# FFN output products: one more seven-product group in each second pass, T2's weight sum moved to an adding DMA, T4's kept on VectorE, products reordered

## The chip, the core and the metric

One core of a Trainium2 chip runs the whole program. The metric is the device time of one execution in microseconds; the median of three runs of the kernel before is 1753.33 us. TensorE is the matrix engine, VectorE and ScalarE work elementwise, GpSimd issues some DMAs, and SyncE (SP in the profile) issues most loads.

## What is computed

A decoder layer on 256 tokens of width 2048 in float32: a SwiGLU FFN, a token mixer, a second SwiGLU FFN. Only the output products of the two FFNs change (`D_FF` = 5504 = 43 k-tiles of 128):

```python
def swiglu_ffn(x, w_in, w_out):
    gate, up = jnp.split(x @ w_in, 2, axis=-1)
    return (jax.nn.silu(gate) * up) @ w_out

x = x + 0.5 * swiglu_ffn(rmsnorm(x, ffn1_norm[l]), ffn1_w_in[l], ffn1_w_out[l])
...
x = x + 0.5 * swiglu_ffn(rmsnorm(x, ffn2_norm[l]), ffn2_w_in[l], ffn2_w_out[l])
```

## The kernel before

**Split numbers.** A float32 product is made of three matmuls of rounded parts: high x high, high x low, low x high. ScalarE copies a weight tile into the ring `whi` (high part), VectorE subtracts it from the original into `wlo` (low part), then TensorE takes both. The same is done with the activations `act` (`act_hi`/`act_lo` into `aw_hi`/`aw_lo`, one k-tile of 128x256; `group_act_hi`/`group_act_lo` for a group's two pairs of tiles). The ring has `SLOTS` = 4 slots (L40) in this stage, so ScalarE's copy for product h waits until TensorE has used product h - 4 (`weights_used`).

**Output stage** (`ffn_out`, once per FFN u = 0, 1). It has two passes c = 0, 1, each over 1024 of the 2048 output columns and all 43 k-tiles. A "plain" item is one k-tile: 2 token blocks x 2 column blocks x 3 = 12 matmuls of 512 columns. Four k-tiles can form a group instead: the 2x2 by 2x2 block product is done with seven products instead of eight (a scheme of Winograd's kind). Each of the seven ("T1", "B11", "T3", "T2", "B21", "B22", "T4") is 2 k-tiles x 3 = 6 matmuls, so a group takes 42 matmuls, four plain tiles 48. The T products need sums of weight blocks (`out_sum`, four 128x1024 operations of VectorE per group), and T1, T2, T3 and B22 need sums of activation blocks (`group_form_sums`, four 128x256 operations, then one copy and one low part of 128x1024, `group_form_hi` and `group_form_lo`). The sums of activations are made in the first pass only and kept in `sfo` for the second one.

**Order.** `out_items` (L65) lists the items of a pass; all three engines walk this list. Both passes have four groups. With P for a plain tile a first pass runs

```text
P P P P P P | T1 B11 P T3 T2 P B21 B22 P T4 P P | T1 B11 ... T4 P P | ... T4 P P P
```

and a second pass has five leading and four trailing P. Work of VectorE between the items is placed by position: `group_form_sums` six items ahead of T1, `group_form_lo` three ahead, `out_sum` T1 two ahead. After the last T4 of a pass, six `join` steps add the separate accumulators onto x (`copy_p1` on ScalarE ahead of them). TensorE starts the second pass after join step 2. In the second FFN the last three plain tiles are done bank by bank, and ahead of them TensorE waits for `aw_ready` of the very last tile (L844).

**Loads.** `out_loads` (L84) orders the loads of weight pieces (1 MB each: two k-tiles of 1024 columns). Plain pieces use three slots, group pieces (two per group, n0 with B11 and B12, n1 with B21 and B22) three others. SyncE's queue is in order; `free` names what must be done before a slot is filled again: for n0 the sum for T4, for n1 the low part of B22. GpSimd's queue carries, in this stage, the reload of x, and at the end of the first FFN the small loads of the mixer. In the FFN input stage GpSimd already issues adding DMAs (`add_piece`, L599).

## Time and profile before

| | |
|---|---|
| median of 3 runs | 1753.33 us (1752.81 to 1753.72) |
| profiled execution | 1753.02 us, span of the profile 1751.2 us |
| TensorE busy | 1742.3 us (99%) |
| VectorE busy | 1473.4 us (84%) |
| ScalarE busy | 1106.5 us (63%) |
| granted TensorE clock | 1.000 of full speed |
| DMA | 405.03 MB, mean 231 GB/s |

The output stages run from 456.4 to 681 us (first FFN) and from 1524 to 1748 us (second FFN). The timeline has a row for an instruction: start, duration, engine, source line, operation, tiles, and in brackets how long the engine was idle before it and what released it. Durations overlap in a pipeline: what an instruction costs its engine is the distance from its start to the next one's.

### The profile page before, as it was taken

To read this page: it belongs to the slowest core of one execution; us is meant where nothing else is said; L and a number is where in the kernel's file an instruction comes from. 1 tells how busy PE (TensorE), PEld (TensorE's weight loads), DVE (VectorE), ACT (ScalarE), POOL (GpSimd) and SP (SyncE) were. 2 spreads that over 40 slices of the span, in tenths; PEclk is the share of its full clock that TensorE was granted. 3 is DMA by queue.
4 is the path that set the end of the run, shared out by engine and by line. 5 is a ranking of instruction groups with operands and counts; after the bars stand their busy time and mean duration, and the time that the engine had idled before them with its cause. 6 is when DMAs were issued, how large, how long until landed. Compare 5 with 4: busy or idle time off the path is not lost.

```text
span 1751.2 us, 21435 instructions
## 1 busy us (share of the span) xinstructions
PE 1742.3 (99%) x7976; PEld 1451.8 (83%) x7976; DVE 1473.4 (84%) x1778; ACT 1106.5 (63%) x1461; POOL 94.9 (5%) x111
## 2 busy tenths in 40 slices
PE   9999999999999999999999999999999999999999
PEld 7888888888888888888888888888888888988887
DVE  7999889998999998575655655898999898899998
ACT  7676666766666666454545554667676676666665
POOL 0000100000000001100000000010000000000000
PEclk9999999999999999999999999999999999999999
DMA  9899899997555556555454558689999898764762
GB/s 378 255 294 275 260 264 265 265 277 236 210 212 201 197 215 210 186 186 178 160 185 161 176 175 298 207 264 263 267 277 278 272 282 239 251 210 159 257 218 90
DMA packets 168327, 405.03 MB, mean 231 GB/s; under 512 B 9016, under 2 KB 18000, under 8 KB 162848
## 3 DMA queue, kind: packets, MB, share of 16 engines
q1 hardware_dynamic: 154208, 342.03, 54.3%
q0 software_dynamic: 12896, 59.67, 17.2%
q10 hardware_dynamic: 1120, 1.97, 0.3%
q8 instruction: 64, 1.05, 0.2%
q14 instruction: 39, 0.32, 0.0%
HBM read 351.57 MB, written 5.79 MB: 204 GB/s over the span
## 4 chain that ended last, share of the span: by engine, by line
PE 95%; DVE 3%; DMA 1%; ACT 0%; issue 0%; SPq 0%; POOL 0%; DVEq 0%; ACTq 0%
PE bank L699 8%; PE bank L700 8%; PE bank L701 8%; PE bank L726 8%; PE bank L728 7%; PE bank L727 7%; PE bank L660 7%; PE bank L662 7%; PE bank L661 7%; PE bank L806 5%; PE bank L808 5%; PE bank L807 5%; PE bank L833 3%; PE bank L834 3%; PE bank L832 3%; DVE wlo L1363 1%
## 5 line engine op out<-in xcount | busy, mean ns | idle before, releaser
L1363 DVE TENSOR_TENSOR wlo<-raw,whi 128x1024 fp32r<-128x1024 f32 (+1 forms) x466 | 559.8, 1208 | 179.4 <-ACT whi L1002 173.6
L1002 ACT ACTIVATE whi<-raw 128x1024 fp32r<-128x1024 f32 (+1 forms) x466 | 486.3, 1047 | 304.1 <-PE bank L662 189.2
L726 PE MATMUL bank<-whi,xs 128*128 128x512 f32 (+1 forms) x528 | 205.6, 389 | 3.0 <-DVE wlo L1363 2.3
L728 PE MATMUL bank<-whi,xs 128*128 128x512 f32 (+1 forms) x528 | 203.1, 385 | 0.0
L727 PE MATMUL bank<-wlo,xs 128*128 128x512 f32 (+1 forms) x528 | 202.9, 384 | 0.0
L806 PE MATMUL bank<-whi,aw_hi 128*128 128x512 f32 x420 | 164.0, 390 | 0.0
L808 PE MATMUL bank<-whi,aw_lo 128*128 128x512 f32 x420 | 163.5, 389 | 0.0
L807 PE MATMUL bank<-wlo,aw_hi 128*128 128x512 f32 x420 | 163.4, 389 | 0.0
L660 PE MATMUL bank<-whi,xs 128*128 128x512 f32 x384 | 155.1, 404 | 0.4 <-DVE wlo L1363 0.4
L662 PE MATMUL bank<-whi,xs 128*128 128x512 f32 x384 | 150.0, 391 | 0.0
L661 PE MATMUL bank<-wlo,xs 128*128 128x512 f32 x384 | 149.5, 389 | 0.0
L1002 ACT ACTIVATE whi<-tsum 128x1024 fp32r<-128x1024 f32 (+1 forms) x96 | 96.9, 1032 | 43.2 <-DMA tmini<-minis 14.8
L1227 ACT ACTIVATE whi<-raw 128x1024 fp32r<-128x1024 f32 x80 | 84.7, 1059 | 61.1 <-PE bank L808 37.0
L726 PEld LDWEIGHTS bank<-whi,xs 128*128 128x128 f32 x528 | 99.2, 188 | 24.6 <-ACT p1s L1170 2.1
L701 PE MATMUL bank<-whi,xs 128*128 128x512 f32 (+1 forms) x312 | 119.3, 382 | 0.0
L699 PE MATMUL bank<-whi,xs 128*128 128x512 f32 (+1 forms) x312 | 119.3, 382 | 0.0
L700 PE MATMUL bank<-wlo,xs 128*128 128x512 f32 (+1 forms) x312 | 119.3, 382 | 0.0
L728 PEld LDWEIGHTS bank<-whi,xs 128*128 128x128 f32 x528 | 99.1, 188 | 19.1
L1363 DVE TENSOR_TENSOR wlo<-tsum,whi 128x1024 fp32r<-128x1024 f32 (+1 forms) x96 | 111.2, 1187 | 3.8 <-ACT whi L1002 3.8
L727 PEld LDWEIGHTS bank<-wlo,xs 128*128 128x128 f32 x528 | 99.4, 188 | 18.0
L699 PE MATMUL bank<-whi,sf 128*128 128x512 f32 (+1 forms) x260 | 99.6, 383 | 0.0
L701 PE MATMUL bank<-whi,sf 128*128 128x512 f32 (+1 forms) x260 | 99.4, 382 | 0.0
(257 smaller groups left out, 3541.6 us busy)
## 6 DMA issues: line engine op xcount, KB each, us to landing
raw<-ffn_w_in SPq DMA_DIRECT2D x86, 1024.0 KB, 6.8
raw<-ffn_w_out SPq DMA_DIRECT2D x84, 1024.0 KB, 6.4
raw<-w_in SPq DMA_DIRECT2D x48, 1024.0 KB, 5.0
raw<-ffn_w_in SPq DMA_DIRECT2D x75, 512.0 KB, 7.4
tsum<-raw POOLq DMA_DIRECT2D x35, 1024.0 KB, 7.9
minis<-ffn_w_in SPq DMA_DIRECT2D x72, 256.0 KB, 7.5
last_plain<-ffn_w_in SPq DMA_DIRECT2D x36, 512.0 KB, 9.3
raw<-w_out SPq DMA_DIRECT2D x16, 1024.0 KB, 5.0
```

Source lines behind the costliest of these rows:

```text
L660: mm(banks[b][:, 0:w], stationary[:, k, 0, tok], hi, start=k == 0, stop=False, skip_group_check=True)
L661: mm(banks[b][:, 0:w], stationary[:, k, 0, tok], lo, start=False, stop=False, skip_group_check=True)
L662: last = mm(banks[b][:, 0:w], stationary[:, k, 1, tok], hi, start=False, stop=k == k_total - 1, skip_group_check=True)
L699: mm(bank_out[:, 0:w], st_hi, hi, start=start, stop=False, skip_group_check=True)
L700: mm(bank_out[:, 0:w], st_hi, lo, start=False, stop=False, skip_group_check=True)
L701: return mm(bank_out[:, 0:w], st_lo, hi, start=False, stop=stop, skip_group_check=True)
L726: mm(banks[b][:, 0:w], xs[:, k + i, 0, tok], hi, start=starts[b] and k + i == 0, stop=False, skip_group_check=True)
L727: mm(banks[b][:, 0:w], xs[:, k + i, 0, tok], lo, start=False, stop=False, skip_group_check=True)
L728: last = mm(banks[b][:, 0:w], xs[:, k + i, 1, tok], hi, start=False, stop=k + i == last_k, skip_group_check=True)
L806: mm(bank_out[:], st_hi, hi, start=i == 0, stop=False, skip_group_check=True)
L1002: A(hi_of(h)[:, 0:n_el], src, ACT.Copy).then_inc(weights_hi, 1)
L1363: V.tensor_tensor(lo_of(h)[:, 0:n_el], src, hi_of(h)[:, 0:n_el].bitcast(f32), ALU.subtract).then_inc(weights_lo, 1)
```

## The change

The second pass of each FFN gets a fifth group (k-tiles 16 to 19, which stay plain tiles in the first pass). Its sums of activations are made in the second pass and take the place of group 0's in `sfo`. The sum for T2 is made by an adding DMA that GpSimd issues, in the buffer that holds the sum for T1 (there are two such buffers, by turns); the sum for T4 is added by VectorE in the same buffer. All weight sums become additions, and the signs move to the sums of activations and to the last join steps. T2 and B22 change places, and T4 of a group is done behind T1 and B11 of the next group. The second pass has no plain tiles between its groups:

```text
first pass, new:   P P P P P P | T1 B11 P T3 B22 P T2 B21 P P P | T1 B11 T4' P T3 B22 P T2 B21 P P P | ... B21 P | T4 P P P
second pass, new:  P P P P P | T1 B11 P T3 B22 P T2 B21 P | T1 B11 T4' P T3 B22 P T2 B21 P | ... five groups ... B21 P | T4 P P P
```

(T4' is the T4 of the group before.) The activations of B11 are split for one token block only, those of B21 and T4 at B22. Slot n0 is free after the low part of T3, n1 after that of T4. The join steps are packed closer together.

```diff
-OUT_GROUPS = (4, 4)
+GROUP_IDS = ((0, 1, 2, 3), (0, 1, 2, 3, 4))
+OUT_GROUPS = tuple(len(ids) for ids in GROUP_IDS)
-LEADS = ((6, 2, 2, 2), (5, 2, 2, 2))
+LEADS, BETWEEN = (6, 5), (2, 0)
+KEPT = 4
+SUMS_AT = [(0, g) for g in range(OUT_GROUPS[0])] + [(1, KEPT)]
...
+        items += [("form", g, "T1"), ("form", g, "B11")] + ([("form", g - 1, "T4")] if g else [])
+        for forms in (("T3", "B22"), ("T2", "B21"), ()):
+            items += [("plain", next(plain))] + [("form", g, f) for f in forms]
+        items += [("plain", next(plain)) for _ in range(BETWEEN[c] if g + 1 < OUT_GROUPS[c] else 0)]
+    return items + [("form", OUT_GROUPS[c] - 1, "T4")] + [("plain", k) for k in plain]
...
+JOIN_FROM = [OUT_ITEMS[c].index(("form", OUT_GROUPS[c] - 1, "T2")) + 4 for c in range(PASSES)]
+JOIN_STEPS = [{JOIN_FROM[0]: (0,), JOIN_FROM[0] + 1: (1, 2)},
+              {JOIN_FROM[1]: (0,), JOIN_FROM[1] + 1: (1, 2), JOIN_FROM[1] + 2: (3,)}]
...
-            at.setdefault(-(-done // 2) + 1 if g else 1, []).append(g)
+            at.setdefault(done // 2 + 2 if g else 1, []).append(g)
...
-                        if q < 2 * OUT_GROUPS[c] and q % 2 == 0:
-                            return out_sums, 4 * group(u, c, q // 2) + 4
-                        item = ("form", q // 2, "B22") if q < 2 * OUT_GROUPS[c] else ("plain", min(2 * q + 1, FT - 1))
+                        item = ("form", q // 2, ("T3", "T4")[q % 2]) if q < 2 * OUT_GROUPS[c] else ("plain", min(2 * q + 1, FT - 1))
...
+            def out_adds(u):
+                for c in range(PASSES):
+                    for g in range(OUT_GROUPS[c]):
+                        G, n1 = group(u, c, g), out_piece(u, c, 2 * g + 1)
+                        pool.wait_ge(weights_lo, out_half(u, c, ("form", g, "T1")) + 1)
+                        pool.wait_ge(raw_full[raw_slot(n1)], RAW_FULL[n1])
+                        pool.dma_start(out_half_sum(G), quarter(n1, 1), accum_op=ALU.add).then_inc(out_t2, 16)
...
             x_again(0)
+            out_adds(0)
...
+                            if f == "T2":
+                                act_e.wait_ge(out_t2, 16 * (G + 1))
+                            if f == "T4":
+                                act_e.wait_ge(out_t4, G + 1)
...
-                            if f in ("T1", "B11"):
-                                group_act_hi(u, c, g, (0,) if f == "T1" else (1,))
+                            if f in ("T1", "B22"):
+                                group_act_hi(u, c, g, 0 if f == "T1" else 1)
...
-                if f == "T2":
-                    dve.wait_ge(out_sums, 4 * G + 2)
-                    dve.wait_ge(weights_lo, out_half(u, c, ("form", g, "B11")) + 1)
-                    V.tensor_tensor(B11, B12, B11, ALU.add).then_inc(out_sums, 1)
                 if f == "T4":
-                    dve.wait_ge(out_sums, 4 * G + 3)
-                    V.tensor_tensor(pair(tsum[:, 2 * W:4 * W]), B21, B11, ALU.subtract).then_inc(out_sums, 1)
+                    dve.wait_ge(weights_lo, out_half(u, c, ("form", g, "T2")) + 1)
+                    V.tensor_tensor(out_half_sum(G), quarter(n1, 0), out_half_sum(G), ALU.add).then_inc(out_t4, 1)
...
-                                if d == (5 if g1 else 3) and c1 == 0:
-                                    group_form_sums(u, 0, g1)
-                                if d == 2 and c1 == 0:
-                                    group_form_lo(u, 0, g1)
+                                if d == (5 if g1 else 3) and (c1, g1) in SUMS_AT:
+                                    group_form_sums(u, c1, g1)
+                                if d == 2 and (c1, g1) in SUMS_AT:
+                                    group_form_lo(u, c1, g1)
```

## Rows read from the trace of the kernel before

**Rows 1.** The page, chain of work that ended last, by engine.
```profile
PE 95%; DVE 3%; DMA 1%; ACT 0%; issue 0%; SPq 0%; POOL 0%; DVEq 0%; ACTq 0%
```

**Rows 2.** Timeline of TensorE, 1714 to 1719 us: start, duration, instruction.
```profile
1715.78 0.39 PE L806 MATMUL bank<-whi,aw_hi 128*128 128x512 f32 x1
...
1718.50 0.39 PE L806 MATMUL bank<-whi,aw_hi 128*128 128x512 f32 x1
```

**Rows 3.** Windows (first and second pass): us, then PE, PEld, DVE, ACT, POOL busy.
```profile
500.00:530.00 30.00, 30.00 (x134) 24.86 (x133) 29.97 (x37) 20.81 (x27) 0.00 (x0) 1.00 0.52 191
600.00:640.00 40.00, 40.00 (x178) 33.12 (x177) 37.71 (x41) 25.84 (x33) 0.00 (x0) 1.00 0.57 210
```

**Rows 4.** Timeline of VectorE and TensorE, first pass, 529 to 546 us.
```profile
529.11 0.42 DVE L1457 TENSOR_TENSOR gset<-act 128x256 f32<-128x256 f32 x1
...
530.58 1.22 DVE L1679 TENSOR_TENSOR wlo<-raw,whi 128x1024 fp32r<-128x1024 f32 x1
...
540.67 0.68 DVE L1445 TENSOR_TENSOR aw_lo<-act,aw_hi 128x512 fp32r<-128x512 f32 x1
541.27 1.22 DVE L1477 TENSOR_TENSOR raw<-raw 128x1024 f32<-128x1024 f32 x1
542.40 1.22 DVE L1679 TENSOR_TENSOR wlo<-raw,whi 128x1024 fp32r<-128x1024 f32 x1
...
544.14 0.42 DVE L1440 TENSOR_TENSOR aw_lo<-act,aw_hi 128x256 fp32r<-128x256 f32 x1
544.48 1.22 DVE L1363 TENSOR_TENSOR wlo<-raw,whi 128x1024 fp32r<-128x1024 f32 x1
...
545.84 0.47 PE L806 MATMUL bank<-whi,aw_hi 128*128 128x512 f32 x1
```

**Rows 5.** Timeline of ScalarE and TensorE: pitch of copies, and a copy behind TensorE.
```profile
547.83 0.40 ACT L1066 ACTIVATE aw_hi<-act 128x256 fp32r<-128x256 f32 x1
548.14 1.05 ACT L1002 ACTIVATE whi<-raw 128x1024 fp32r<-128x1024 f32 x1
...
1718.95 0.39 PE L808 MATMUL bank<-whi,aw_lo 128*128 128x512 f32 x1
...
1719.43 1.06 ACT L1227 ACTIVATE whi<-raw 128x1024 fp32r<-128x1024 f32 x1 [1.66 <-PE bank L808]
```

**Rows 6.** Timeline of all engines at the end of the last pass, 1728 to 1740.
```profile
1728.56 0.58 ACT L1086 ACTIVATE p1s<-bank 128x512 f32<-128x512 f32 x1
...
1730.32 1.06 ACT L1227 ACTIVATE whi<-tsum 128x1024 fp32r<-128x1024 f32 x1 [1.18 <-PE bank L808]
...
1731.41 1.23 DVE L1679 TENSOR_TENSOR wlo<-tsum,whi 128x1024 fp32r<-128x1024 f32 x1 [1.44 <-ACT whi L1227]
...
1738.16 1.28 DVE L1495 SCALAR_TENSOR_TENSOR x<-bank,x 128x512 f32<-128x512 f32 x2
...
1739.35 0.39 PE L808 MATMUL bank<-whi,aw_lo 128*128 128x512 f32 x1
1739.36 0.41 DVE L1440 TENSOR_TENSOR aw_lo<-act,aw_hi 128x256 fp32r<-128x256 f32 x1
...
1739.83 0.50 PE L861 MATMUL bank<-whi,aw_hi 128*128 128x512 f32 x1
```

**Rows 7.** Adding DMAs of GpSimd in the input stages: issues, and landing of L603.
```profile
L603 POOL DMA_DIRECT2D tsum<-raw x37: 847/856/940, 71.5 to 1489.5; - x37
...
DMA to landing us min/median/max: 5.6/7.9/9.7
...
tsum<-raw POOLq DMA_DIRECT2D x35, 1024.0 KB, 7.9
...
tmini<-minis POOLq DMA_DIRECT2D x35, 256.0 KB, 9.4
...
1284.73 0.86 POOL L603 DMA_DIRECT2D tsum<-raw  x1 [22.46 <-DVE wlo L1369]
1285.27 1.20 POOL L604 DMA_DIRECT2D tmini<-minis  x1
```

**Rows 8.** Weight loads issued between 562 and 570 us, time to landing.
```profile
DMA to landing us min/median/max: 7.7/9.1/10.5
```

**Rows 9.** Timeline of VectorE behind the first FFN's output stage.
```profile
679.87 1.66 DVE L1379 SCALAR_TENSOR_TENSOR xs<-bank,gains,xs 128x256 fp32r<-128x256 f32 x4 [3.71 <-ACT xs L1022]
```

More of the change, by code:

```diff
@@ L53 @@
 FIRST_OUT_SLOT = 2
-OUT_GROUPS = (4, 4)
+GROUP_IDS = ((0, 1, 2, 3), (0, 1, 2, 3, 4))
+OUT_GROUPS = tuple(len(ids) for ids in GROUP_IDS)
 OUT_PLAIN = [4 * g for g in OUT_GROUPS]
-FORMS = ("T1", "B11", "T3", "T2", "B21", "B22", "T4")
-LEADS = ((6, 2, 2, 2), (5, 2, 2, 2))
+LEADS, BETWEEN = (6, 5), (2, 0)
+KEPT = 4
+SUMS_AT = [(0, g) for g in range(OUT_GROUPS[0])] + [(1, KEPT)]
 def out_items(c):
-    items, plain = [], iter(range(OUT_PLAIN[c], FT))
+    plain = iter(range(OUT_PLAIN[c], FT))
+    items = [("plain", next(plain)) for _ in range(LEADS[c])]
     for g in range(OUT_GROUPS[c]):
-        items += [("plain", next(plain)) for _ in range(LEADS[c][g])]
-        for forms in (("T1", "B11"), ("T3", "T2"), ("B21", "B22"), ("T4",)):
-            items += [("form", g, f) for f in forms]
-            if forms != ("T4",):
-                items.append(("plain", next(plain)))
-    return items + [("plain", k) for k in plain]
+        items += [("form", g, "T1"), ("form", g, "B11")] + ([("form", g - 1, "T4")] if g else [])
[3 more added lines that the diff above has]
+    return items + [("form", OUT_GROUPS[c] - 1, "T4")] + [("plain", k) for k in plain]
 OUT_ITEMS = [out_items(c) for c in range(PASSES)]
@@ L78 @@
 OUT_AT = [0, OUT_LEN[0]]
-T4_ENDS = [OUT_ITEMS[c].index(("form", OUT_GROUPS[c] - 1, "T4")) for c in range(PASSES)]
+JOIN_FROM = [OUT_ITEMS[c].index(("form", OUT_GROUPS[c] - 1, "T2")) + 4 for c in range(PASSES)]
+JOIN_STEPS = [{JOIN_FROM[0]: (0,), JOIN_FROM[0] + 1: (1, 2)},
+              {JOIN_FROM[1]: (0,), JOIN_FROM[1] + 1: (1, 2), JOIN_FROM[1] + 2: (3,)}]
 ACT_PLAIN = [ACT_PAIRS - 2 * g for g in OUT_GROUPS]
@@ L169, in raw_slot @@
     if n >= IN_P[1]:
-        return (0, 2, 1, 3, 4, 5, 0, 1)[n - IN_P[1]]
+        oldest = (FIRST_OUT_SLOT - sum(ACT_PLAIN) - (IN_P[1] - QKV_P)) % QKV_RAW_SLOTS
+        return (*((oldest - i) % QKV_RAW_SLOTS for i in range(3)), 3, 4, 5, 0, 1)[n - IN_P[1]]
     return (FIRST_OUT_SLOT - sum(ACT_PLAIN) - (n - QKV_P)) % QKV_RAW_SLOTS if n >= QKV_P else n % RAW_SLOTS
@@ L376, in split_sums, with out_half_sum, kept @@
         def split_sums(g):
-            return sfo[:, 4 * g:4 * g + 4]
-        def kept(u, g):
-            return OUT_GROUPS[1] * u + g + 1
+            return sfo[:, 4 * (g % KEPT):4 * (g % KEPT) + 4]
+        def out_half_sum(G):
+            return pair(tsum[:, 2 * W * (G % 2):2 * W * (G % 2 + 1)])
+        def kept(u, c, g):
+            last = max(i for i, (c1, g1) in enumerate(SUMS_AT) if (c1, g1) <= (c, g) and g1 % KEPT == g % KEPT)
+            return len(SUMS_AT) * u + last + 1
         p_banks = [bank[0:4], bank[4:8]]
@@ L1070, in group_act_hi @@
                     c0, g0 = (c, g - 1) if g else (c - 1, OUT_GROUPS[0] - 1)
[L1071 removed]
+                    act_e.wait_ge(weights_used, out_half(u, c0, ("form", g0, ("B11", "T4")[part])) + 1)
                 else:
                     act_e.wait_ge(weights_used, unit_half(u, UNITS - 1) + B22 + 2)
[L1074 to L1076 removed]
+                t, cols = 4 * GROUP_IDS[c][g] + 2 * part, (P, SEQ)[part]
+                act_e.wait_ge(act_copied, ACT_PAIRS * u + t // 2 + 1)
+                A(aw_hi[:, 2 + part, :, 0:cols], act[:, t:t + 2, 0:cols], ACT.Copy).then_inc(ga_hi, 1)
             def group_form_hi(u, c, g):
[L1079 to L1080 removed]
+                act_e.wait_ge(weights_used, out_half(u, c, ("form", g - KEPT, "T2")) + 1 if g >= KEPT else OUT[u])
+                act_e.wait_ge(gs_summed, 4 * kept(u, c, g))
                 A(split_sums(g)[:, :, :, 0, :], gs[c], ACT.Copy).then_inc(gs_hi, 1)
@@ L1209, in ffn_out @@
                         if len(ahead) > 3 and ahead[3][0] == "form" and ahead[3][2] == "T1":
-                            if c == 0 and i + 3 < OUT_LEN[0]:
-                                group_form_hi(u, 0, ahead[3][1])
+                            if (c, ahead[3][1]) in SUMS_AT and i + 3 < OUT_LEN[c]:
+                                group_form_hi(u, c, ahead[3][1])
                         if item[0] == "plain":
@@ L1675, in ffn_out @@
                             n0, n1 = out_piece(u, c, 2 * g), out_piece(u, c, 2 * g + 1)
-                            src = {"T1": pair(tsum[:, 0:2 * W]), "B11": quarter(n0, 0), "T3": quarter(n0, 1), "T2": quarter(n0, 0),
-                                   "B21": quarter(n1, 0), "B22": quarter(n1, 1), "T4": pair(tsum[:, 2 * W:4 * W])}[f]
+                            own = out_half_sum(group(u, c, g))
+                            src = {"T1": own, "B11": quarter(n0, 0), "T3": quarter(n0, 1), "T2": own,
+                                   "B21": quarter(n1, 0), "B22": quarter(n1, 1), "T4": own}[f]
                             dve.wait_ge(weights_hi, h + 1)
```

82 lines of the change are left out of this document (38 added, 44 removed).

## Prediction

> **What bounds the kernel now.** I read the chain of waits first: 95% of the time to the end is TensorE work [rows 1], so only fewer products, or a wait of TensorE, can move the time. The page's mean of one matmul (0.389 us) is no price: matmuls overlap. The timeline gives it: twelve matmuls of 512 columns start in 2.72 us (1715.78 to 1718.50), 0.2267 us each [rows 2]. A plain k-tile (12 matmuls) is 2.72 us of TensorE, a form product (6) 1.36 us.
>
> Then I asked who is nearly late. In the windows of the output stage TensorE is busy without a break, but VectorE nearly is too: 29.97 of 30 us in the first pass, 37.71 of 40 in the second [rows 3]. The timeline of VectorE gives the prices, by the distance from one start to the next [rows 4]: a 128x1024 operation (a low part, or a sum of weights) 1.13 us (541.27 to 542.40), the activations' low part of a plain tile 0.34 (544.14 to 544.48), that of 128x512 0.60 (540.67 to 541.27), the four sums of activations 1.47 (529.11 to 530.58). In a first-pass group of five plain tiles and seven forms VectorE has 12 low parts (13.6), 5 x 0.34, 2 x 0.60, 4 sums of weights (4.5), 1.47 and 1.13 for the sums of activations: 23.6 us, against 5 x 2.72 + 7 x 1.36 = 23.1 on TensorE. It loses half a microsecond per group, and in the fourth its lead is used up: the low part begun at 544.48 ends at 545.70, and the matmul that needs it starts at 545.84 and is the slow first one, 0.47 us [rows 4]. No time is lost there yet, but the stage has no slack that a denser order could use.
>
> How far may VectorE run ahead? ScalarE may copy into a ring slot when TensorE has used the product four before it. Such a copy starts 0.25 us after the next product began (last matmul of the product started at 1718.95, so the next product at 1719.18, and the copy at 1719.43) [rows 5]; the low part starts 1.09 us after the copy (1730.32, 1731.41) [rows 6] and takes 1.22. So a low part is ready 2.5 to 2.6 us after the product four before it, if VectorE is free.
>
> **The change part by part.**
> (a) The fifth group: four k-tiles (48 matmuls) become seven forms (42). Two second passes: 12 matmuls fewer, 12 x 0.2267 = **-2.72 us**.
> (b) T2's sum leaves VectorE: -1.13 us per group there, worth nothing by itself, since TensorE did not wait. First pass: 23.6 - 1.13 - 0.26 (the first group copy is half as wide) = 22.2 against 23.1: the tight place at 545.84 goes, and no time with it.
> (c) The second pass has no plain tiles between its groups any more. A group is 3 plain tiles and 7 forms: TensorE 8.16 + 9.52 = 17.7 us. VectorE: 10 low parts 11.3, 3 x 0.34, 0.34 + 0.60, 3 sums 3.4: 16.7. It fits, at 94%. But group 4 was not summed in the first pass. Its sums (1.47) and their low part (1.13) fall inside group 3: 19.3 against 17.7. I follow the one stretch in which VectorE has no gap. It starts behind the low part of B21 of group 2, which is ready 2.5 us after the product four before it (T3 of group 2) is used. From there VectorE does: sum T1, sum T4, low parts of plain, T1, B11, T4, plain, T3, sum T3 (9 x 1.13 = 10.2) and three small ones (1.0), 11.2 in all; then the sums of activations 1.47, low parts B22, plain, T2, the form sums, B21, sum T1, sum T4, plain (8 x 1.13 = 9.1), 0.60 and two of 0.34: 11.8. With 0.2 for the end of the last one and the hand-over: 2.5 + 11.2 + 11.8 + 0.2 = 25.7 us. TensorE meanwhile has B22, plain, T2, B21, plain, T1, B11, T4, plain, T3, B22, plain, T2, B21: 10 forms and 4 plain, 13.6 + 10.9 = 24.5, and wants the last plain tile of group 3. **It waits 1.3 us, in each of the two stages: +2.6.**
> (d) The end. Before its last section (three tiles, bank by bank) TensorE waits for the activations' low part of the very last tile. Before, TensorE had T4 and a plain tile to do in front of it, and still waited: last matmul at 1739.35, the next due at 1739.58, that low part begun at 1739.36, matmul at 1739.83, 0.25 us [rows 6]. Now T4 stands last and the plain tile in front of it is gone. After T2 of group 4 is used: 0.25, ScalarE's copy of P1 (0.5 of its 0.58 us [rows 6]), the tile's activations 0.31 (547.83 to 548.14 [rows 5]), the copy, 2.1 us to VectorE's low part; then 1.13, join 0.60, 0.34, 1.13, three joins 1.8 (two took 1.20 from 1738.16 to 1739.36 [rows 6]), 0.42: 7.6. TensorE has B21, plain, T4: 5.4. Wait 2.2, less the 0.25 of before: **+1.9**, once, in the second FFN. In the first, the next work needs no such wait, and VectorE, which stood idle for 3.71 us before 679.87 [rows 9], takes the same lateness out of that cover; without it, it would cost up to the same 1.9.
> (e) T2's sum as a DMA. GpSimd waits for T1's low part and the piece's landing; behind it on its queue stand only the next sums and, in the first FFN, the small loads of the mixer, not due for some 30 us. ScalarE's copy of T2 waits for the landing, and all later copies with it. No half-size adding DMA is in the trace. From above: 1 MB landed in 7.9 us (5.6 to 9.7), an issue 0.86 [rows 7]; from below, 256 KB more landed about 2 us later (issue 0.54 after, 9.4 to land), so 8 us per MB and perhaps 4 for half. I take 6. The window: T2's copy is due when the plain tile behind B11 is used; from T1's gate to that are 5 forms and 2 plain, 12.2 us, plus 0.25, less 2.6 for T1's own low part and about 0.8 of VectorE's queue: 9 us. Cost 0, as long as it lands within 9 us; the whole measured span but its end does.
> (f) Loads. The group's second piece is held until T4's low part, three products into the next group; its first one is freed at T3. SP's queue is in order, so the plain piece behind them waits too. The first piece is used 8 us after T3, the second 11 or more; loads landed in 7.7 to 10.5 us where several were queued [rows 8]. Three in a row are issued from 1.4 us before T3. I take 0 and keep +1 per stage.
>
> The profiled execution took 1753.02 us (span 1751.2 and 1.8 around it), 0.3 under the median: -2.72 + 2.6 + 1.9 = +1.8, so 1754.8 on it, and **1755.1** on the median of 1753.33.
>
> A page's rule against (e): the Trainium skill ("SBUF — State Buffer", who interferes with whom) says that a VectorE instruction with two SBUF inputs excludes a GpSimd instruction that reads SBUF. In the units GpSimd's issues beside a busy VectorE took 0.86 us each [rows 7]; no row shows one beside a VectorE at 100%. Another page ("DMA: Bandwidth & Descriptors", anatomy of one DMA) gives 2 us + bytes/436 GB/s, an estimate of 3.2 us for 512 KB; for the 1 MB of [rows 7] it would give 4.4, and the trace says 7.9. By either figure the sum stays.
>
> **The rivals.**
> *Only the products count*: VectorE makes up the 1.3 and the 1.9 somewhere, because a stretch that I took as gapless is shorter. For it: none of 16 groups of before lost time, and (b) gives VectorE 1.13 per group. Against it: both are sums of one queue's own durations. 1753.3 - 2.7 = 1750.6; with one of the two waits 1752 to 1753.
> *The adding DMA is late* (slower). It decides from a landing 9 to 10 us after T1's low part. Behind T2's gate VectorE has T2, B21, two sums and a plain tile, 6.0 us and 1.4 for the copy, TensorE 8.2: 0.8 us of slack in second-pass groups. At 11 us, 2 late, each of 10 groups loses 1.2: 12 us, 1767. At 10, some 2 us: 1757. For it: the 9.7 of [rows 7], loads beside it, and the rule on SBUF above. Against: half the bytes.
> *Loads late in the dense pass*: +1 to +1.5 per stage, 1757 to 1758. For it: the 10.5 of [rows 8].
> *More than the products is gained*: the 0.25 of the end and stalls that I can't see go: below 1749.8.
>
> **How the numbers follow.** A run of this kernel can tell 0.2% (3.5 us) from no change. Forecast 0.55 (own range 1753.8 to 1756.8); products only 0.16; DMA late 0.14; loads late 0.11; more gained 0.04. Faster than 1749.8: 0.04. Slower than 1756.8: most of the late DMA and of the late loads and the forecast's edge, 0.12 + 0.09 + 0.05 = 0.26. The rest, 0.70, is within. The range: 1750.3 (products only, less 0.3) to 1759.5 (loads late, or a DMA at 10.3 us), leaving out 0.05 below and 0.1 above.
>
> **What would show it.** (a) 12 matmuls fewer, starts still 0.2267 us apart. (c) in each second pass one gap on TensorE of about 1.3 us in front of the plain tile that follows B21 of group 3, released by VectorE's low part, VectorE without a gap for 23 us ahead of it. (d) a gap of 2.2 us in front of the last section, released by the activations' low part. (e) the adding DMA of 512 KB lands in 4 to 8 us and ScalarE never waits for it. (b) VectorE under 29 of 30 us in the first pass. I am wrong if gaps stand in front of T2 or in every group (then the DMA or the loads), or if those two gaps are missing.

## The result, and the profile after

The changed kernel takes 1761.05 us (median of 6 executions, 1758.86 to 1764.51), the kernel before 1753.53 beside it: 1.0046 times as long, 95% interval 1.0032 to 1.0059. The forecast was 1755.1 with a range to 1759.5. The profiled execution took 1759.58 us (span 1757.3, clock 1.000), so by its own sum the prediction (1754.8 on the profiled execution) is 4.8 us short, and the median lies another 1.5 above. The result is outside the range, on the slow side.

The page of the changed kernel, busy times (us, share of the span, count), then the chain that ended last by engine:

```profile
PE 1740.6 (99%) x7964; PEld 1449.5 (82%) x7964; DVE 1470.4 (84%) x1780; ACT 1111.4 (63%) x1465; POOL 116.5 (7%) x129
...
PE 88%; DVE 7%; DMA 3%; issue 1%; ACT 1%; SPq 0%; POOL 0%; DVEq 0%; ACTq 0%
```

TensorE has 12 matmuls fewer (7976 before) and is busy for less time than before (1742.3 us); the span is 6.1 us longer. The chain, 95% TensorE before [rows 1], is now 88% TensorE, 7% VectorE and 3% DMA (3% and 1% before). So TensorE waits. The page of waits says for what:

```profile
PE bank L825 <- DVE wlo L1386: 5.9, 4, 1.7
...
PE bank L880 <- DVE aw_lo L1463: 2.0, 1, 2.0
```

Four waits for a plain tile's low part, one for the activations' low part in front of the last section. The timeline of TensorE, each time the last matmul ahead of a gap and the one behind it (start, duration, instruction, idle and releaser); 0.2267 us is the step from start to start without a gap [rows 2]:

```profile
649.07 0.39 PE L853 MATMUL bank<-whi,aw_lo 128*128 128x512 f32 x1
650.74 0.47 PE L825 MATMUL bank<-whi,aw_hi 128*128 128x512 f32 x1 [1.28 <-DVE wlo L1386]
...
1663.31 0.39 PE L853 MATMUL bank<-whi,aw_lo 128*128 128x512 f32 x1
1665.31 0.47 PE L825 MATMUL bank<-whi,aw_hi 128*128 128x512 f32 x1 [1.61 <-DVE wlo L1386]
...
1700.57 0.39 PE L853 MATMUL bank<-whi,aw_lo 128*128 128x512 f32 x1
1702.64 0.47 PE L825 MATMUL bank<-whi,aw_hi 128*128 128x512 f32 x1 [1.68 <-DVE wlo L1386]
...
1720.20 0.39 PE L853 MATMUL bank<-whi,aw_lo 128*128 128x512 f32 x1
1721.94 0.47 PE L825 MATMUL bank<-whi,aw_hi 128*128 128x512 f32 x1 [1.35 <-DVE wlo L1386]
...
1743.60 0.39 PE L853 MATMUL bank<-whi,aw_lo 128*128 128x512 f32 x1
1745.94 0.50 PE L880 MATMUL bank<-whi,aw_hi 128*128 128x512 f32 x1 [1.96 <-DVE aw_lo L1463]
```

The time lost is the distance of the two starts less 0.2267. Three of the five were forecast, with their places: 650.74 (1.44 us) and 1721.94 (1.51) for the last plain tile of group 3, and 1745.94 (2.11) for the last section. Two were not: 1665.31 (1.77) and 1702.64 (1.84), both in the second FFN only. "DVE wlo" as releaser hides their cause; VectorE's own timeline has it:

```profile
1661.34 1.23 DVE L1496 TENSOR_TENSOR tsum<-raw 128x1024 f32<-128x1024 f32 x1 [2.07 <-DMA raw<-ffn_w_out]
1662.48 1.22 DVE L1503 TENSOR_TENSOR tsum<-raw,tsum 128x1024 f32<-128x1024 f32 x1
1663.61 0.42 DVE L1463 TENSOR_TENSOR aw_lo<-act,aw_hi 128x256 fp32r<-128x256 f32 x1
1663.95 1.22 DVE L1386 TENSOR_TENSOR wlo<-raw,whi 128x1024 fp32r<-128x1024 f32 x1
...
1698.66 1.23 DVE L1496 TENSOR_TENSOR tsum<-raw 128x1024 f32<-128x1024 f32 x1 [2.15 <-DMA raw<-ffn_w_out]
```

VectorE stands idle for 2.07 and 2.15 us in front of the sum for T1 of the next group, because the group's first piece has not landed. Behind that sum stand T4's sum and the low part of the plain tile, and TensorE wants that plain tile first. The loads are issued by SyncE three in a row; the view of line L491 for the stretches 1648 to 1656 and 1688 to 1696 us:

```profile
L491 SPq DMA_DIRECT2D raw<-ffn_w_out x3: 367/368/469, 1651.6 to 1652.7; - x3
...
DMA to landing us min/median/max: 7.0/9.3/11.1
...
L491 SPq DMA_DIRECT2D raw<-ffn_w_out x3: 368/368/403, 1689.0 to 1690.1; - x3
...
DMA to landing us min/median/max: 6.2/9.2/11.0
```

The order in the queue is a plain piece, the group's first piece, its second. The middle one, issued at 1651.97, lands 9.3 us later, at 1661.31: that is when the sum starts. VectorE was ready for it 7.3 us after the issue (7.0 us at the second place). Groups 1 and 3 have such a triple; for groups 2 and 4 the plain piece came earlier. The first FFN's second pass has the same two triples; there the middle load landed in 7.3 and 7.2 us, and VectorE did not wait.

### The profile page after: what moved, and what is told of

The parts are those of the page before. It is cut to its first block, busy times and chain, and to the rows that moved or that the text cites. A ratio compares the mean times of both kernels' runs of the same rounds, so it can differ in the third digit from the quotient of the medians.

```text
span 1757.3 us, 21439 instructions
## 1 busy us (share of the span) xinstructions
PE 1740.6 (99%) x7964; PEld 1449.5 (82%) x7964; DVE 1470.4 (84%) x1780; ACT 1111.4 (63%) x1465; POOL 116.5 (7%) x129
## 3 DMA queue, kind: packets, MB, share of 16 engines
q8 instruction: 64, 1.05, 0.2%
## 4 chain that ended last, share of the span: by engine, by line
PE 88%; DVE 7%; DMA 3%; issue 1%; ACT 1%; SPq 0%; POOL 0%; DVEq 0%; ACTq 0%
PE bank L718 8%; PE bank L720 8%; PE bank L719 8%; PE bank L745 8%; PE bank L747 7%; PE bank L746 7%; PE bank L679 7%; PE bank L681 7%; PE bank L680 7%; PE bank L825 4%; PE bank L827 4%; PE bank L826 4%; PE bank L853 2%; PE bank L852 2%; PE bank L851 2%; DMA raw<-ffn_w_out 2%
## 5 line engine op out<-in xcount | busy, mean ns | idle before, releaser
L1386 DVE TENSOR_TENSOR wlo<-raw,whi 128x1024 fp32r<-128x1024 f32 (+1 forms) x458 | 549.6, 1206 | 183.7 <-ACT whi L1021 177.4
L1021 ACT ACTIVATE whi<-raw 128x1024 fp32r<-128x1024 f32 (+1 forms) x458 | 477.7, 1046 | 326.5 <-PE bank L681 189.2
L825 PE MATMUL bank<-whi,aw_hi 128*128 128x512 f32 x388 | 151.7, 391 | 5.9 <-DVE wlo L1386 5.9
L827 PE MATMUL bank<-whi,aw_lo 128*128 128x512 f32 x388 | 151.1, 389 | 0.0
L826 PE MATMUL bank<-wlo,aw_hi 128*128 128x512 f32 x388 | 151.0, 389 | 0.0
L719 PE MATMUL bank<-wlo,sf 128*128 128x512 f32 (+1 forms) x260 | 99.4, 382 | 0.0
```

Of the source, the lines that this page charges most:

```text
L719: mm(bank_out[:, 0:w], st_hi, lo, start=False, stop=False, skip_group_check=True)
L825: mm(bank_out[:], st_hi, hi, start=i == 0, stop=False, skip_group_check=True)
L1021: A(hi_of(h)[:, 0:n_el], src, ACT.Copy).then_inc(weights_hi, 1)
L1386: V.tensor_tensor(lo_of(h)[:, 0:n_el], src, hi_of(h)[:, 0:n_el].bitcast(f32), ALU.subtract).then_inc(weights_lo, 1)
```

## The experiments

**Four groups in both passes** (`e1_four`), the rest of the change kept.

```diff
-GROUP_IDS = ((0, 1, 2, 3), (0, 1, 2, 3, 4))
+GROUP_IDS = ((0, 1, 2, 3), (0, 1, 2, 3))
-LEADS, BETWEEN = (6, 5), (2, 0)
+LEADS, BETWEEN = (6, 5), (2, 2)
-SUMS_AT = [(0, g) for g in range(OUT_GROUPS[0])] + [(1, KEPT)]
+SUMS_AT = [(0, g) for g in range(OUT_GROUPS[0])]
```

> The changed kernel without the fifth group: four groups in both passes, two plain tiles between groups, and all the rest of the change kept (adding DMA for T2, T4 behind the next group's B11, the new load order). It computes the whole layer. Theory of density (the time was lost because the second pass lost its plain tiles between groups, and with them the time for loads and for VectorE): no gap of TensorE in the output stages over 0.3 us, 1753.0 to 1753.8 us, as the kernel before. Rival (the adding DMA or the late T4 costs the time by itself, wherever it stands): gaps in front of T2 or behind it in every group, 1757 or more.

Measured: 1755.97 us (1754.38 to 1757.42), before 1753.4; ratio 1.0013 [1.0003, 1.0022]. That is neither theory. The gaps for loads and those of group 3 are gone, so the fifth group and the dense order together make them; which part makes which, the next runs show. But three things remain, all in the second FFN, here in the timelines of ScalarE and TensorE:

```profile
1548.89 1.06 ACT L1250 ACTIVATE whi<-tsum 128x1024 fp32r<-128x1024 f32 x1 [4.40 <-DMA tsum<-raw]
...
1739.95 0.39 PE L827 MATMUL bank<-whi,aw_lo 128*128 128x512 f32 x1
1742.25 0.50 PE L880 MATMUL bank<-whi,aw_hi 128*128 128x512 f32 x1 [1.91 <-DVE aw_lo L1463]
...
1742.82 0.61 PE L882 MATMUL bank<-whi,aw_lo 128*128 128x512 f32 x1
1743.23 0.63 PE L880 MATMUL bank<-whi,aw_hi 128*128 128x512 f32 x1
```

First, the second FFN's first adding DMA landed 12.5 us after its issue; ScalarE stood 4.4 us, TensorE lost 1.3 in two gaps (0.29 and 0.97). Second, the gap in front of the last section is here too (2.07 us), so the fifth group is not what makes it. A plain tile does stand between T4 and the last section here, and VectorE does two more joins (1740.58 to 1741.78) ahead of the low part. Third, behind that gap the matmuls start 0.41 to 0.43 us apart, which is the 1.2 GHz level of the clock in place of 2.4: from 1742.82 on eight of them, about 8 x 0.2 = 1.6 us more. (Where such a stretch fills a window, the profile says so itself: a granted clock of 0.52 in `e4_join` from 1665.2 to 1668.3 us, 0.50 in `e5_vector` from 1672 to 1675.) In the changed kernel's profiled execution the same gap, 2.11 us, had no such stretch behind it.

**Old sums** (`e2_oldsums`): group 4 takes the sums of activations that group 0 left; its own sums, their copy and their low part are left out, so the output is not the layer's.

```diff
-SUMS_AT = [(0, g) for g in range(OUT_GROUPS[0])] + [(1, KEPT)]
+SUMS_AT = [(0, g) for g in range(OUT_GROUPS[0])]
```

> The changed kernel with group 4 of each second pass using the sums of activations that group 0 left (its own four sums, their copy and their low part are left out; everything else runs as before). Theory of my ledger (c): the gap in front of the plain tile behind B21 of group 3 goes in both stages (1.44 and 1.51 us in the profile), the other gaps stay, about 3.0 us faster than the changed kernel: 1758 on its median, 1756.6 on its profiled execution. Rival (that gap is made by loads like the two others): it stays, and the time with it.

Measured: 1757.28 (1755.21 to 1760.29), profiled span 1753.3. TensorE's gaps for group 3 (649 and 1720 us before) are gone, in both stages; those for loads (1.61 and 1.60) and the last section (2.12) stay. So step (c) is right in its cause: the sums of activations and their low part, 2.6 us of VectorE, in the dense group.

**Early loads** (`e3_early`): in the second pass a group's loads are issued one plain piece earlier.

```diff
-            at.setdefault(done // 2 + 2 if g else 1, []).append(g)
+            at.setdefault(done // 2 + (1 if c else 2) if g else 1, []).append(g)
```

> The changed kernel with the loads of the groups 1 to 4 of the second pass put one plain piece earlier in SyncE's order. Theory of late loads (the first piece of groups 1 and 3 stands behind a plain piece and in front of another, and lands 9 us or more after its issue): VectorE's waits of 2.1 us for the piece (sum for T1) go, and with them the gaps of 1.77 and 1.84 us in the second FFN; the gaps of 1.5 (group 3's last plain tile) and 2.1 (end) stay: 1756 on the quietest executions and a spread of under 2 us between executions. Rival (VectorE's crowding makes these gaps, the load only comes last by chance): gaps of over 1 us stay at these places.

Measured: 1756.29 (1753.95 to 1758.29), profiled span 1752.9. Both gaps for loads are gone, and VectorE's sum for T1 waits for no load. The timelines of VectorE and TensorE at the first of the two places:

```profile
1658.78 1.22 DVE L1496 TENSOR_TENSOR tsum<-raw 128x1024 f32<-128x1024 f32 x1
...
1662.92 0.39 PE L853 MATMUL bank<-whi,aw_lo 128*128 128x512 f32 x1
1663.15 0.39 PE L825 MATMUL bank<-whi,aw_hi 128*128 128x512 f32 x1
```

The load of that piece was no faster (10.3 us), but it was issued at 1641.11 and landed at 1651.44, 7 us ahead of the sum. The other gaps stand: 1.2 us each for group 3, 2.12 at the end. This is the kernel that the prediction described, and its median and its profiled execution (1755.11) are near the forecast. The spread of under 2 us that I expected did not come: it is 4.3 us, and six of the ten executions have a granted clock of 0.999.

**Late joins** (`e4_join`): the joins 1, 2 and 3 of the last pass stand behind the activations' low part of the last tile.

```diff
-              {JOIN_FROM[1]: (0,), JOIN_FROM[1] + 1: (1, 2), JOIN_FROM[1] + 2: (3,)}]
+              {JOIN_FROM[1]: (0,), JOIN_FROM[1] + 2: (1, 2, 3)}]
```

> The changed kernel with join steps 1 and 2 of the second pass put behind the last low part. Theory of my ledger (d): the activations' low part of the last tile starts 1.8 us earlier, the gap in front of the last section falls from 2.1 to about 0.3 us, and the time by 1.8 us; three updates of x wait longer but end under the last section. Rival (the end is held by the last weight tile's copies or the joins come to the end of the chain instead): 0 to 0.8 us.

Measured: 1760.07 (1758.61 to 1763.44, 4 executions). The median alone shows nothing; the place does. In front of the last section 0.32 us is left of 2.11 (starts 1744.63 and 1745.18). But the wait for a load at 1662 was longer in this profiled execution, and behind it the clock fell; the timeline of TensorE:

```profile
1662.31 0.39 PE L853 MATMUL bank<-whi,aw_lo 128*128 128x512 f32 x1
1665.16 0.77 PE L825 MATMUL bank<-whi,aw_hi 128*128 128x512 f32 x1 [2.47 <-DVE wlo L1386]
1665.73 0.63 PE L826 MATMUL bank<-wlo,aw_hi 128*128 128x512 f32 x1
1666.15 0.63 PE L827 MATMUL bank<-whi,aw_lo 128*128 128x512 f32 x1
...
1667.86 0.55 PE L825 MATMUL bank<-whi,aw_hi 128*128 128x512 f32 x1
1668.25 0.39 PE L826 MATMUL bank<-wlo,aw_hi 128*128 128x512 f32 x1
```

A gap of 2.6 us, then 0.42 to 0.43 us per matmul until 1668: together 2.85 + 3.09 us for what takes 1.8 at full speed.

**T2's sum on VectorE** (`e5_vector`), no adding DMA in the output stages.

```diff
-            out_adds(0)
...
-                                act_e.wait_ge(out_t2, 16 * (G + 1))
+                                act_e.wait_ge(out_t2, G + 1)
...
+                if f == "T2":
+                    dve.wait_ge(weights_lo, out_half(u, c, ("form", g, "T1")) + 1)
+                    V.tensor_tensor(out_half_sum(G), quarter(n1, 1), out_half_sum(G), ALU.add).then_inc(out_t2, 1)
...
+                        if i > 1 and OUT_ITEMS[c][i - 1][-1] == "B11":
+                            out_sum(u, c, OUT_ITEMS[c][i - 1][1], "T2")
```

> T2's sum is made by VectorE again (one operation of 128x1024 behind the low part of B11, in T1's buffer), and GpSimd issues no adding DMA; all else as after. If VectorE is what limits the second pass, each of its groups now needs 16.7 + 1.13 = 17.8 us of VectorE against 17.7 of TensorE, and group 3 19.3 + 1.13 = 20.4: TensorE's gap in front of the plain tile behind B21 of group 3 grows from 1.4 to 1.5 us by one to four operations of 1.13, in both stages, so +2.3 to +8 us: 1763 to 1769. Rival, the adding DMAs cost more than they save (issues on GpSimd, traffic beside the loads): the time falls below that of after, 1761.05, and the loads of the second FFN land sooner than in 7 us (median).

Measured: 1767.91 (1766.92 to 1770.8), ratio 1.0084 [1.007, 1.0098]. 6.9 us more than the change, within the bounds, but not where I expected it: the gap of group 3 grew only to 1.6 us in both stages, while gaps of 0.25 to 0.6 came in front of other plain tiles, and the two for loads in the second FFN grew to 2.5 and 2.4. VectorE is what limits the second pass, and the adding DMA is worth its price in the dense order. The loads landed in 5.1 and 5.8 us (medians of the two stages) instead of 6.0 and 7.3, as the rival said, but that buys less than it costs.

**One plain tile between group 3 and group 4** (`e7_gap`), four leading instead of five.

```diff
-LEADS, BETWEEN = (6, 5), (2, 0)
+LEADS, BETWEEN = (6, 4), ((2, 2, 2, 0), (0, 0, 0, 1, 0))
...
-        items += [("plain", next(plain)) for _ in range(BETWEEN[c] if g + 1 < OUT_GROUPS[c] else 0)]
+        items += [("plain", next(plain)) for _ in range(BETWEEN[c][g])]
```

> Second pass with four leading plain tiles (five in after) and one plain tile between group 3 and group 4, so that group 4's sums of activations have 2.72 us more of TensorE work beside them; all else as after. If VectorE's crowding in group 3 is the cause of the gaps of 1.44 and 1.51 us, both go: about 2.9 less than after, median 1758.2; the waits for a load in the second FFN and the 2.1 in front of the last section stay. Rival, the lateness is only moved: a gap of over 1 us stands behind B21 of another group and the median stays within 1 us of 1761.05.

Measured: 1761.38 (1761.0 to 1761.72): nothing gained. The two gaps of group 3 shrank to 0.2, as the theory says, but others came, and the rival's signs are all there: gaps of over 1 us in front of the plain tile behind B21 of other groups (1.09 at 611 us, 2.07 at 1663, 1.05 at 1684) and a median within 1 us of the change's. The view of GpSimd's line L625 from 1640 to 1650 us and TensorE's timeline:

```profile
L625 POOL DMA_DIRECT2D tsum<-raw x1: 1185/1185/1185, 1643.7 to 1643.7; - x1
...
DMA to landing us min/median/max: 14.2/14.2/14.2
```
```profile
1657.96 0.39 PE L827 MATMUL bank<-whi,aw_lo 128*128 128x512 f32 x1
1660.36 0.47 PE L851 MATMUL bank<-whi,sfo 128*128 128x512 f32 x1 [2.01 <-DVE wlo L1698]
```

The adding DMA took 14.2 us, and TensorE lost 2.2 us in front of T2: the rival of the late DMA, at the start of the last pass. With one leading tile fewer, group 0 of this pass comes 2.7 us sooner, into the two stores of the output's first half (issued at 1644.88 and 1650.32) and the loads; which of the two holds the DMA up was not tried. The gap at 1663 followed 12 matmuls later, and behind it the clock fell to its lower level; those at 611 and 1684 stand behind waits of VectorE for a load (1.39 and 1.35 us).

**All three remedies** (`e6_best`): the plain tile of `e7_gap`, the early loads and the late joins.

> The three remedies at once: the plain tile between group 3 and group 4, the second pass's group loads one plain piece earlier, and the joins 1, 2 and 3 of the last pass behind the activations' low part of the last tile. If the gaps of TensorE are all of what the change lost, the 12 matmuls remain: 1753.4 - 2.7 + 0.1 = 1750.8 median, no gap over 0.5 us in either output stage, clock 1.000. The stage's first adding DMA, which landed in 9.8 to 12.5 us in all executions so far, may still cost 0 to 1.3 us in the second FFN: up to 1752. Rival, the gaps were cover for one another: what stood behind the removed ones now limits, and the median is above 1753.4.

Measured: 1751.39 (1750.73 to 1752.02, 11 executions) against 1753.75, ratio 0.9987 [0.9978, 0.9996]. The interval lies below 1, though the difference of 2.4 us is less than the 0.2% that the prediction took as measurable. With early loads the adding DMA that was late in `e7_gap` lands in 7.0 us, and the largest gap in either stage is that of the last section; windows of 640 to 660 us (us, PE, PEld, DVE, ACT, POOL busy, clock), first of the change, then of this kernel:

```profile
640.00:660.00 20.00, 18.72 (x83) 15.19 (x82) 20.00 (x23) 13.54 (x17) 1.21 (x1) 1.00 0.55 174
```
```profile
640.00:660.00 20.00, 19.95 (x89) 16.20 (x88) 19.98 (x22) 13.50 (x19) 1.21 (x1) 1.00 0.52 169
...
1737.51 0.39 PE L853 MATMUL bank<-whi,aw_lo 128*128 128x512 f32 x1
1738.07 0.51 PE L880 MATMUL bank<-whi,aw_hi 128*128 128x512 f32 x1 [0.17 <-DVE aw_lo L1463]
```

VectorE is as full in both, but in the second one TensorE does six matmuls more. The median is 0.6 us above the 1750.8 expected: four gaps of 0.2 to 0.3 us are left (at 647, 1553, 1713 and 1738 us), 1.3 us with the slow steps behind them.

**And the first group's T2 on VectorE** (`e8_first`): as `e6_best`, without the stage's first adding DMA.

```diff
+                        if c == 0 and g == 0:
+                            continue
...
+                        if c == 0 and i > 1 and OUT_ITEMS[c][i - 1] == ("form", 0, "B11"):
+                            out_sum(u, c, 0, "T2")
```

> As the kernel with the three remedies, and besides the T2 sum of the very first group of each stage is made by VectorE (behind B11), so that no adding DMA is issued beside the full queue of loads at the stage's start. If that DMA (landing 9.8 to 12.5 us against 4.8 for the others) costs TensorE 0.2 to 1.3 us at times, this one is 0 to 1 us below the kernel with the three remedies and its executions spread less: 1750.6 to 1751.2. If not, the same median within 0.3 us, or VectorE's 1.13 us in the first group shows as a gap there.

Measured: 1751.48 (1750.85 to 1752.95). The small gap at 1553 us (0.18) went, the median did not move. With the DMA landing in about 11 us, as here, it costs next to nothing.

**The change again** (`e9_again`), for time and clock.

> The changed kernel itself, unchanged, for more executions beside their granted clock. If stretches of TensorE at half its clock behind the longer gaps make the difference between its profiled execution (1759.6) and its median (1761.05), then executions with a clock of 1.000 take 1758.5 to 1760, and those with 0.998 some 3.5 us more (0.002 x 1760), 1762 to 1764.5. If the landing of loads alone makes the difference, time and clock are not related.

Measured: 1762.31 (1759.49 to 1766.77). Together with the first comparison there are eleven executions. With a granted clock of 1.000: 1758.86, 1759.49, 1759.58, 1759.59, 1759.85. With 0.999: 1762.31, 1762.5. With 0.998: 1762.74, 1764.25, 1764.51. With 0.997: 1766.77. So the quiet execution is 1759.5, and the 1.5 us up to the median and the spread go with the clock. They are not all clock: 0.003 of 1760 us is 5.3 us, and the slowest execution is 7.3 above the quiet one; longer waits may stand beside it, as in `e4_join`, but the slow executions have no trace. That the clock falls behind the gaps is shown only where a trace caught it (`e1_four`, `e4_join`, `e5_vector`, `e7_gap`, `e13_swap`).

**Two remedies** (`e10_two`): early loads and late joins, group 3 as crowded as in the change.

> Two remedies of three: the second pass's group loads one plain piece earlier and the late joins; the crowding of VectorE in group 3 is left alone. If the terms add, this is the kernel with all three remedies (1751.4) plus the two gaps of group 3 (1.2 to 1.5 us each): 1753.8 to 1754.4. Rival, the crowding costs nothing once the loads are early: 1751.4 to 1752.

Measured: 1753.46 (1752.92 to 1754.1). This is 0.3 under the bounds. The two gaps of group 3 are there (1.23 us each) and the difference to `e6_best` is 2.1 us: the terms add (2 x 1.23, less the 0.2 that `e6_best` keeps at each of the two places). Against `e3_early`, which differs only by the gap of 2.1 us in front of the last section, the median is 2.8 us lower (before ran in 1753.6 beside the one and 1753.4 beside the other), 1.0 more than the 1.8 that the gap shrinks by; all ten executions have a clock of 1.000 and they spread over 1.2 us instead of 4.3. So of these three gaps the longest, and not the two of 1.23, goes with the clock's falls.

**Remedies with T2 on VectorE** (`e11_vec`): the edit of `e5_vector` in `e6_best`.

> All three remedies, but T2's sum by VectorE and no adding DMA in the output stages. VectorE then has 17.8 us per second-pass group against 17.7 of TensorE, 20.4 against 20.4 in group 3, and 23.3 against 23.1 in a first-pass group. If VectorE's load is what counts, gaps of some tenths come back in most groups: 1 to 3.5 us more than 1751.4, 1752.4 to 1755. Rival, the adding DMA is worth nothing here: 1751.4 within 0.5.

Measured: 1755.93 (1755.09 to 1756.94), 4.5 us more than with the adding DMA, a little over my bound. Thirteen waits of 0.2 to 0.6 us stand in the two second passes, all in front of a plain tile, and the loads land in 5.7 and 6.5 us against 6.0 and 7.0 in `e6_best`, so faster loads are little of it either way. Without the adding DMA this kernel, fifth group and all remedies included, is 2.3 us slower than the kernel before.

**Four groups with late joins** (`e12_four2`): `e1_four` with the joins 1, 2 and 3 behind the last tile's low part.

> Four groups in both passes, with two plain tiles between groups, the late joins, and the rest of the change (order, T2's sum by the adding DMA, T4's by VectorE). It has as many matmuls as the kernel before. If order and DMA bring nothing by themselves and the 12 matmuls are the whole gain, it takes the time of before plus 0.1 to 0.5 us, and up to 1.3 more where the stage's first adding DMA is late: 1753.6 to 1755. Rival, the order itself costs TensorE time elsewhere: over 1755.5, as the kernel with four groups and the early joins.

Measured: 1752.38 (1751.9 to 1752.91), ratio 0.9994 [0.9985, 1.0003], 1.2 us less than before with the same number of matmuls. The interval takes in 1, so the difference is small against its error, though the slowest of its ten executions (1752.91) is faster than the fastest of the 27 of before (1753.12). I had expected more than before. The kernel before has small gaps in its first passes (at 533, 545, 1600 and 1612 us) and the one at its end (1739), 0.96 us together with the slow steps behind them, and none of them is left here. They were the tight places of [rows 4]: a matmul that comes just late costs 0.04 to 0.09, and the step behind it takes 0.31 instead of 0.23. The rest of the difference no gap shows.

This kernel also says what the fifth group is worth. It has the same order, DMA and late joins as `e6_best` without the fifth group, and it takes 1752.38 us against 1751.39: the 12 matmuls fewer bring 1.0 us of their 2.72, mostly because the dense passes keep gaps of 1.3 us that this kernel has not.

**Whose loads are slow** (`e13_swap`): each FFN's output stage reads the other's `w_out`.

```diff
-                w_out = io[f"ffn{u + 1}_w_out"][0].rearrange("(t p) d -> p t d", p=P)
+                w_out = io[f"ffn{2 - u}_w_out"][0].rearrange("(t p) d -> p t d", p=P)
```

> The changed kernel, but each FFN's output stage reads the other FFN's w_out (same shape and layout, other values; the output therefore is that of exchanged weights). If the loads of the second FFN land later (7.3 us against 6.0, median) because of where its w_out lies, the two medians change places, the sum T1 waits for a load in the second pass of the first FFN and the waits at 1661 and 1698 us vanish. If it is the stage's own traffic and order of events, the medians and the two waits stay where they are and the time stays 1759 to 1765.

Measured: 1761.11 (1759.14 to 1763.19). The view of DMA issues in the two output stages (KB, median us to landing), first of the change, then of this kernel:

```profile
raw<-ffn_w_out SPq DMA_DIRECT2D x37, 1024.0 KB, 6.0
...
raw<-ffn_w_out SPq DMA_DIRECT2D x37, 1024.0 KB, 7.3
```
```profile
raw<-ffn_w_out SPq DMA_DIRECT2D x37, 1024.0 KB, 7.0
...
raw<-ffn_w_out SPq DMA_DIRECT2D x37, 1024.0 KB, 6.0
```

The two medians changed places. New gaps came in the first FFN (at 632 us 1.83), and those of the second one shrank (1.77 to 0.89, 1.84 to 0.65) without going away. The kernel before shows the same difference between its two stages, 5.0 and 6.7 us. So the slower landing belongs to the tensor. It is not the whole cause of the second FFN's two gaps, since VectorE still waits 1.19 and 0.96 us for its loads there with the faster tensor. Why one of two equal tensors is slower no view shows.

**Stores moved away** (`e14_store`): the stores of the output's first half go behind items 48 and 51 of the last pass.

> The changed kernel, but the two stores of 1 MB of the output's first half, which ScalarE issues behind items 6 and 9 of the last pass (1644 to 1652 us), are issued behind items 48 and 51 (some 85 us later). If these stores are what delays the three loads issued at 1651.6 to 1652.7, their landing falls from 7.0/9.3/11.1 us toward the first FFN's 4.9/7.3/7.8 and TensorE's gap of 1.8 us at 1663 goes, while the one at 1700, 37 us behind the stores, stays: about 1.8 us less on an execution with a clock of 1.000 (1757.7). If the stores don't matter, both gaps stay.

Measured: 1761.65 (1759.44 to 1762.59). The medians stayed (6.0 and 7.3); the triple behind the old place of the stores landed in 6.6/8.7/10.5 instead of 7.0/9.3/11.1, and its gap fell from 1.77 to 1.12, while the later one stayed (1.80). In the first FFN, which has no such stores, this profiled execution has a gap of 0.59 at 632 us that the change's own had not, so 0.6 us is no more than two executions may differ by. The stores are not what makes the gap: 1.1 us of it stays without them. A share of 0.6 us they may have.

## Why the prediction failed, step by step

The sum against the profiled execution was +1.8; measured is +6.56. Each term from the change's timeline, gaps with the slow step behind them (0.08 each, 0.11 at the last section):

| step | predicted | measured |
|---|---|---|
| (a) 12 matmuls | -2.72 | -2.72 |
| (b) small gaps of before go | 0 | -0.61 (0.36 more is in d) |
| (c) crowding in group 3 | +2.6 | +3.1 |
| (d) last section | +1.9 | +1.9 (2.11 + 0.11 - 0.36) |
| (e) adding DMA | 0 | +0.24 |
| (f) loads | 0 | +3.77 |
| rest, not explained: 0.4 around the span, 0.5 in it | 0 | +0.9 |
| from the profiled execution to the median | +0.3 | +1.5 |

**(f) is the step that failed.** The prediction had the mechanism ("the plain piece behind them waits too", "Three in a row are issued") and a rival with the price of +1 to +1.5 per stage, and still put 0 into the sum, where the runs have 3.77 us. The need was written beside it, 8 us for the group's first piece, and [rows 8] has two loads, one of 10.5 and one of 7.7 us (the 9.1 is only their mean): by its own numbers a piece could come 2.5 us late. Three more errors hid the size: the need was 7.0 to 7.3 us and not 8, it counted one wait per stage where two groups of five have a triple, and it took the landing times from the first FFN alone. For the first FFN 0 was right, by a hair (7.3 and 7.2 us); the second FFN's loads are slower by 1.3 us in the median (1.7 before), which the kernel before already shows, and its two triples landed in 9.3 and 9.2. `e3_early` shows that the term is the loads: issued earlier, both gaps are gone, and the median of 1756.29 lies in the range.

**The clock was left out.** Every price in the sum was taken at full clock. The change makes five gaps of 1.4 to 2.1 us where there was one of 0.25, and where a trace caught the clock falling, it was behind gaps of 2.1 to 2.6 us. In the eleven executions 1.5 us of the median and a spread of 8 us go with it, most of it clock and a part not known. The kernel before lies within 3 us, the repaired one within 1.3.

**(c) and (d) held,** in place, releaser and nearly in size. In (d) the plain tile that is gone, which the prediction names first, does not decide by itself: `e1_four` has one there again and the same gap, since two more joins come ahead of the low part. The joins in front of it decide, and `e4_join` moves them away. In (c) the sum is 0.1 off (25.7 less 24.5 is 1.2, and `e3_early` has 1.23). The prediction counted 23.0 us of VectorE without a break, from the sum for T1 to the plain tile's low part; in the second FFN the sum starts at 1698.66 and the next operation behind that low part at 1721.71, 23.05 us later, with no idle time in between. The end of the stretch:

```profile
1715.70 1.22 DVE L1489 TENSOR_TENSOR sfo<-gset,sfo 128x1024 fp32r<-128x1024 f32 x1
1716.84 1.22 DVE L1698 TENSOR_TENSOR wlo<-raw,whi 128x1024 fp32r<-128x1024 f32 x1
1717.97 1.22 DVE L1496 TENSOR_TENSOR tsum<-raw 128x1024 f32<-128x1024 f32 x1
1719.11 1.22 DVE L1503 TENSOR_TENSOR tsum<-raw,tsum 128x1024 f32<-128x1024 f32 x1
1720.24 0.42 DVE L1463 TENSOR_TENSOR aw_lo<-act,aw_hi 128x256 fp32r<-128x256 f32 x1
1720.58 1.22 DVE L1386 TENSOR_TENSOR wlo<-raw,whi 128x1024 fp32r<-128x1024 f32 x1
```

Four steps of 1.13 to 1.14 and one of 0.34: the pitches of [rows 4] again. `e2_oldsums` takes (c) away, `e4_join` takes (d) away, and nothing else with them.

**(b)** was right for VectorE in direction (windows of the first and the second pass, as in [rows 3])

```profile
500.00:530.00 30.00, 30.00 (x134) 24.86 (x133) 29.40 (x38) 21.58 (x28) 1.20 (x1) 1.00 0.82 290
600.00:640.00 40.00, 40.00 (x178) 33.08 (x177) 38.22 (x44) 28.39 (x36) 2.40 (x2) 1.00 0.75 242
```

(29.40 of 30 us where it was 29.97, though not under the 29 I named) and wrong in "no time with it": the first passes of before lose 0.61 us at four tight places that I had called no loss, and neither the change nor `e12_four2` has them.

**(e)** came out within its bounds of 4 to 8 us but for the first DMA of each stage and one of 8.1. The view of line L625 in the second FFN's output stage:

```profile
L625 POOL DMA_DIRECT2D tsum<-raw x9: 1176/1185/1195, 1537.1 to 1723.2; - x9
...
  ACT whi L1250: 3.2, 1
...
DMA to landing us min/median/max: 4.8/4.8/11.3
```

4.8 us is the median where I took 6 (6.2 to 8.1 us beside several loads), and ScalarE waits once, for the stage's first one, which takes 11.3 us beside the full queue of loads. "ScalarE never waits for it" was wrong; the cost of 0.24 us is small because VectorE and TensorE still had work. The exclusion of which the Trainium skill speaks ("SBUF — State Buffer", "Who interferes with whom") is one between VectorE's two-input instructions and GpSimd instructions that read SBUF; the same section reports that `tensor_tensor`, which VectorE runs here, did not stall DMAs. The trace agrees with the second: no delay of these DMAs shows, 4.8 us is the median with VectorE busy for 38.22 of 40 us in the second pass. The estimate of 3.2 us from the Trainium skill's page "DMA: Bandwidth & Descriptors" ("Anatomy of one DMA") was too low for 512 KB, as the 4.4 was for 1 MB.

The rivals: "only the products count" is out, the gaps are there. "Loads late" was true together with the forecast, not instead of it. Its 1757 to 1758 was already the forecast with 2 to 3 us added, the right mechanism with a chance of 0.11, and still 3 us or more under the median: the term was 3.77, and the clock was in neither.

## What to carry to other kernels

A term that the text itself calls late belongs in the sum at what its rows say, not at 0 with a rival beside it; and a rival that is the forecast with one term more is a question of that term's size, to be settled from the rows, not a chance to be weighed. In an order where one engine has no slack, every wait of that engine for a load comes out on the path: give the load its worst landing of all stages, not the median of the nearest one. A gain from fewer products was hidden behind five gaps of three causes (loads, group 3, the last section), and 1751.4 us came out when each was removed in its own place: 2.4 us under the kernel before, of which the fifth group's fewer products are 1.0 and the rest came without them (`e12_four2`).

## What the runs showed of the hardware that I had not expected

- TensorE's clock can fall to its lower level (starts 0.43 us apart instead of 0.23) behind a gap of 2.1 to 2.6 us, and each such stretch costs about 1.6 us more. It is not certain: of nine gaps of 2.07 to 2.12 us in front of the last section, in the profiled executions of eight kernels (the change twice), three had such a stretch behind them; of three waits for a load with gaps of 2.4 to 2.6 us (`e4_join`, `e5_vector`) two had.
- Loads of 1 MB from one of two tensors of equal shape landed 0.5 to 1.7 us later, in the median, in every kernel here, whichever stage read it.
- An adding DMA of 512 KB lands in 4.8 us in most cases when no load is issued beside it, in up to 10.2 beside several loads, in 9.7 to 12.5 at a stage's start, and in 14.2 once at the start of a last pass with stores and loads under way.
